# Inverse roots of two norms as columns on GpSimd, spread back by a product with ones, in a two-block transformer kernel

## What is computed

```python
# first block: after the two attentions (8 heads of 64 each)
y = jnp.concatenate([rmsnorm(merge(ya, DIL_WIDTH), g_out_dil[l]),
                     rmsnorm(merge(yb, MOBA_WIDTH), g_out_moba[l])], axis=-1)
h = h + y @ w_out[l]

# second block, in each of three mixers (layer 0 for c and x, layer 1 for x)
def layer_norm(x, g, b):
    mu = jnp.mean(xf, axis=-1, keepdims=True)
    var = jnp.mean(jnp.square(xf - mu), axis=-1, keepdims=True)
    y = (xf - mu) * lax.rsqrt(var + EPS)
    return (y * g + b).astype(x.dtype)

def conformer_conv(a, conv_w, conv_b, norm_g, norm_b, w_o):
    gl = a[..., :CONV_WIDTH_2] * jax.nn.sigmoid(a[..., CONV_WIDTH_2:])
    y = conv(gl, 31 taps per channel) + conv_b
    y = jax.nn.silu(layer_norm(y, norm_g, norm_b))
    return y @ w_o
```

## Time and profile before

| | |
|---|---|
| median of 3 runs | 2044.1 us |
| the profiled execution | 2042.34 us |
| its span, first to last instruction | 2040.5 us |
| mean granted TensorE clock | 0.992 of full speed |
| PE busy | 1979.1 us, 97% |
| DVE busy | 1657.4 us, 81% |
| ACT busy | 1114.2 us, 55% |
| GpSimd busy | 142.7 us, 7% |
| the chain that ended last | PE 72%, issue 14%, DVE 9%, ACT 5% |

### The profile page before, as it was taken

One profiled execution on the slowest core, in us unless ns is written; L12 is line 12 of the kernel. 1 busy time (PEld: TensorE's weight loads), 2 busy tenths in 40 slices (PEclk: granted clock), 3 DMA queues, 4 the chain that ended last, 5 costly groups with the idle time before them and its releaser, 6 DMA issues.

```text
span 2040.5 us, 29620 instructions
## 1 busy us (share of the span) xinstructions
PE 1979.1 (97%) x11323; PEld 1694.8 (83%) x11323; DVE 1657.4 (81%) x2464; ACT 1114.2 (55%) x1535; POOL 142.7 (7%) x258
## 2 busy tenths in 40 slices
PE   7999989999999999999999999999999999998998
PEld 6877889988878778888778888888888887787886
DVE  5877779888989987988987888877888889876665
ACT  5555454455674365577347645454665773365553
POOL 4000000000004000002300000000000013000000
PEclk9999999999999999999999999999999999998999
DMA  8635476677656656556656676777766566554653
GB/s 268 202 123 193 153 221 207 196 234 236 206 169 195 201 171 214 183 156 190 211 168 203 200 247 229 239 244 227 249 221 194 176 190 203 186 187 126 213 177 123
DMA packets 196716, 404.64 MB, mean 198 GB/s; under 512 B 15767, under 2 KB 18067, under 8 KB 196576
## 3 DMA queue, kind: packets, MB, share of 16 engines
q1 hardware_dynamic: 187888, 387.50, 59.8%
q0 software_dynamic: 8688, 15.25, 2.5%
HBM read 396.74 MB, written 1.10 MB: 195 GB/s over the span
## 4 chain that ended last, share of the span: by engine, by line
PE 72%; issue 14%; DVE 9%; ACT 5%; DMA 1%; POOL 0%; DVEq 0%; POOLq 0%; ACTq 0%
PE gps L1229 13%; PE gps L1231 13%; PE gps L1230 13%; PE gps L1253 6%; PE gps L1236 4%; PE gps L1237 4%; PE gps L1238 4%; PE gps L1255 3%; DVE wlo L2163 2%; PE gps L1213 2%; PE aps L1165 2%; PE aps L1131 2%; ACT whi L1634 1%; PE aps L1005 1%; PE aps L1118 1%
## 5 line engine op out<-in xcount | busy, mean ns | idle before, releaser
L2163 DVE TENSOR_TENSOR wlo<-raw,whi 128x1024 fp32r<-128x1024 f32 (+1 forms) x648 | 760.6, 1186 | 238.9 <-ACT whi L1634 236.1
L1634 ACT ACTIVATE whi<-raw 128x1024 fp32r<-128x1024 f32 (+1 forms) x648 | 660.6, 1027 | 529.1 <-PE gps L1231 377.8
L1229 PE MATMUL gps<-whi,both 128*128 128x512 f32 x1624 | 649.1, 400 | 6.8 <-DVE wlo L2163 6.6
L1231 PE MATMUL gps<-whi,both 128*128 128x512 f32 x1624 | 634.1, 390 | 0.0
L1230 PE MATMUL gps<-wlo,both 128*128 128x512 f32 x1624 | 633.9, 390 | 0.0
L1229 PEld LDWEIGHTS gps<-whi,both 128*128 128x128 f32 x1624 | 305.6, 188 | 79.9 <-DVE wlo L2163 11.6
L1231 PEld LDWEIGHTS gps<-whi,both 128*128 128x128 f32 x1624 | 305.5, 188 | 65.4
L1230 PEld LDWEIGHTS gps<-wlo,both 128*128 128x128 f32 x1624 | 305.8, 188 | 60.5
L1236 PE MATMUL gps<-both,whi 128*128 128x256 f32 x960 | 276.1, 288 | 1.5 <-DVE wlo L2163 1.5
L1237 PE MATMUL gps<-both,whi 128*128 128x256 f32 x960 | 271.7, 283 | 0.0
L1238 PE MATMUL gps<-both,wlo 128*128 128x256 f32 x960 | 271.6, 283 | 0.0
(11 more groups left out here) (314 smaller groups left out, 1759.9 us busy)
## 6 DMA issues: line engine op xcount, KB each, us to landing
raw<-w_in SPq DMA_DIRECT2D x232, 512.0 KB, 4.3
raw<-w_ff SPq DMA_DIRECT2D x192, 512.0 KB, 4.6
raw<-ada_wT SPq DMA_DIRECT2D x96, 512.0 KB, 4.4
raw<-w_attn_o SPq DMA_DIRECT2D x24, 512.0 KB, 4.3
raw<-w_gmlp_o SPq DMA_DIRECT2D x24, 512.0 KB, 3.8
raw<-w_conv_o SPq DMA_DIRECT2D x24, 512.0 KB, 3.8
raw<-w_out SPq DMA_DIRECT2D x24, 512.0 KB, 4.7
raw<-w_gate SPq DMA_DIRECT2D x20, 512.0 KB, 4.9
```

The source lines that it names most:

```text
L1229: mm(om, ah, whi[:, q, i, :], start=first, stop=False)
L1231: t = mm(om, al, whi[:, q, i, :], start=False, stop=last)
L1634: A_(part(whi, jb, q), raw_part(jb, q), ACT.Copy).then_inc(hi_done[q], 1)
L2163: tt(part(wlo, jb, q), raw_part(jb, q), f32(part(whi, jb, q)), ALU.subtract).then_inc(lo_done[q], 1)
```

## The change

The inverse root is taken on columns: PE forms the sums with the squares as the stationary side and two columns of ones as the moving side, so that a row's sum lands on its own partition; DVE adds EPS; GpSimd takes the power -0.5 of two columns (one per 128 rows); DVE writes two diagonal matrices from them (times D); and PE's product of the ones matrix with the diagonals spreads the values over all partitions again, into PSUM, from where DVE's scalings read them. In the first block `ynD` (diagonals) and `ynB` (spread and scaling) are new steps and `ynL` moves; in the mixers `ln_dg` and `ln_bc` are new, and the chain's steps from `ln_mu` to the last `ln_lo` lie later by a unit or two. One semaphore, `root_step`, counts four steps per root.

```diff
@@ make_plan, first block
         put(hosts[2], 2, "ynS", half=group)
         put(hosts[2], 3, "ynM", half=group)
-    put(j_km0, 2, "ynL", slot=2, half=0)
+        put(hosts[2], 3, "ynD", half=group)
+    put(j_km0, 0, "ynB", half=0)
+    put(j_km0, 1, "ynL", slot=2, half=0)
...
-    put(j_oa[0], 1, "ynL", slot=2, half=1)
+    put(j_oa[0], 1, "ynB", half=1)
+    put(j_oa[0], 2, "ynL", slot=2, half=1)
@@ mixer
-        lm = put(bg[1], 2, "ln_mu", l=l, cks=cks, rb_free=("t_pe", t_g, 4, 4))
-        put(bg[1], 3, "ln_mean", of=lm)
-        put(gates[4], 1, "ln_var", of=lm)
-        put(gates[4], 2, "ln_norm", of=lm)
+        lm = put(bg[1], 3, "ln_mu", l=l, cks=cks, rb_free=("t_pe", t_g, 4, 4))
+        put(gates[4], 0, "ln_mean", of=lm)
+        put(gates[4], 2, "ln_var", of=lm)
+        put(gates[4], 3, "ln_norm", of=lm)
+        put(gates[4], 3, "ln_dg", of=lm)
+        put(gates[5], 0, "ln_bc", of=lm)
         lo = []
-        for h, (at_out, at_mul, at_hi, at_lo) in enumerate((((gates[4], 2), (gates[4], 3), (gates[4], 3), (gates[5], 0)),
-                                                            ((gates[5], 0), (gates[5], 1), (gates[5], 1), (gates[5], 2)))):
+        for h, (at_out, at_mul, at_hi, at_lo) in enumerate((((gates[4], 3), (gates[5], 0), (gates[5], 0), (gates[5], 1)),
+                                                            ((gates[5], 1), (gates[5], 2), (gates[5], 2), (gates[5], 3)))):
@@ GpSimd
+            def root(k):
+                pool.wait_ge(sem["root_step"], 4 * k + 1)
+                nc.gpsimd.tensor_tensor(st[:, 15, 2:4], st[:, 15, 0:2], half_power[:], ALU.pow).then_inc(sem["root_step"], 1)
@@ TensorE, yn_sum
-                for k in range(4):
-                    t = mm(aps[:, 2, 0:S], ones[:], AB[:, k * S:(k + 1) * S], start=k == 0, stop=k == 3)
+                for m in range(2):
+                    for k in range(4):
+                        t = mm(aps[:, 2, 2 * m:2 * m + 2], AB[:, k * S + m * P:k * S + m * P + P], ones[:, 0:2],
+                               start=m == 0 and k == 0, stop=m == 1 and k == 3, skip_group_check=True)
                 t.then_inc(sem["yn_ss"], 1)
+            def spread(diagonals):
+                for m in range(2):
+                    t = mm(aps[:, 2, m * P:m * P + P], ones[:], diagonals[:, m * P:m * P + P], start=m == 0, stop=m == 1,
+                           skip_group_check=True)
+                return t
+            def yn_spread(p):
+                free(p)
+                pe.wait_ge(sem["root_step"], 4 * p.half + 3)
+                spread(GB).then_inc(sem["root_step"], 1)
@@ TensorE, ln_norm
-                ln_total(p, 1).then_inc(sem["ln_vs"], 1)
+                wait(pe, ev("ln_pc", p.of, 2, 2))
+                for m in range(2):
+                    t = mm(aps[:, 2, S + 2 * m:S + 2 * m + 2], PTb[:, 3 * S + m * P:3 * S + m * P + P], ones[:, 0:2], start=m == 0,
+                           stop=m == 1, skip_group_check=True)
+                t.then_inc(sem["ln_vs"], 1)
+            def ln_spread(p):
+                pe.wait_ge(sem["root_step"], 4 * p.of.n + 11)
+                spread(PTb).then_inc(sem["root_step"], 1)
@@ VectorE, first block
+            def diagonals(to):
+                for m in range(2):
+                    t = ts(to[:, m * P:m * P + P], ident[:], st[:, 15, 2 + m:3 + m], float(D), ALU.mult, ALU.mult)
+                return t
+            def yn_mean(p):
+                dve.wait_ge(sem["yn_ss"], p.half + 1)
+                ts(st[:, 15, 0:2], aps[:, 2, 0:4:2], 2.0, EPS, ALU.mult, ALU.add).then_inc(sem["root_step"], 1)
+            def yn_diagonals(p):
+                dve.wait_ge(sem["tp_st"], 16)
+                dve.wait_ge(sem["root_step"], 4 * p.half + 2)
+                diagonals(GB).then_inc(sem["root_step"], 1)
             def yn_scale(p):
-                ts(x, aps[:, 2, 0:S], 2.0 * CUBIC, EPS * CUBIC, ALU.mult, ALU.add).then_inc(sem["yn_ms"], 1)
-                dve.wait_ge(sem["yn_ms"], p.half + 1)
-                rsqrt(rs, x, t_)
+                dve.wait_ge(sem["root_step"], 4 * p.half + 4)
                 for k in range(4 * p.half, 4 * p.half + 4):
                     y = RB[:, k * S:(k + 1) * S]
-                    t = stt(y, y, C1[:, 16 + k:17 + k], rs, ALU.mult, ALU.mult)
+                    t = stt(y, y, C1[:, 16 + k:17 + k], aps[:, 2, 0:S], ALU.mult, ALU.mult)
@@ VectorE, mixers
             def ln_norm(p):
                 wait(dve, ev("ln_vs", p.of))
-                link(ts(x, aps[:, 2, S:2 * S], CUBIC, EPS * CUBIC, ALU.mult, ALU.add))
-                rsqrt(r, x, t_)
+                ts(st[:, 15, 0:2], aps[:, 2, S:S + 4:2], EPS, None, ALU.add).then_inc(sem["root_step"], 1)
+            def ln_diagonals(p):
+                dve.wait_ge(sem["root_step"], 4 * p.of.n + 10)
+                diagonals(PTb).then_inc(sem["root_step"], 1)
+            def ln_scale(p):
+                dve.wait_ge(sem["root_step"], 4 * p.of.n + 12)
+                r = aps[:, 2, 0:S]
                 for half in range(2):
                     y = tiles(Yc[:, half * 4 * S:(half + 1) * 4 * S], 4)
                     tt(y, y, r.unsqueeze(1).to_broadcast([P, 4, S]), ALU.mult).then_inc(sem["ln_n"], 1)
...
-            LATE = ("conv", "ynM", "rq", "rk", "gv_rms", "gv_norm", "final")
+            LATE = ("conv", "ynM", "ynD", "ln_dg", "rq", "rk", "gv_rms", "gv_norm", "final")
```

More of the change, by code:

```diff
@@ L573, in make_plan @@
             elif k == "ynM":
-                use(p, (2,), ("yn_ms", None, 0, p.half + 1))
+                use(p, (2,), ("root_step", None, 0, 4 * p.half + 1))
+            elif k == "ynB":
+                use(p, (2,), ("yn_y", None, 0, p.half + 1))
             elif k == "ma":
@@ L651 @@
 pn_ss pn_e pn_w po_e po_w pn_xn pn_xa t_pe t_hi t_lo
-ba_s ba_sb ba_nm ba_p ba_pn ba_tp ba_pt ba_pv ba_y yn_sq yn_ss yn_ms yn_y yn_hi yn_lo
+ba_s ba_sb ba_nm ba_p ba_pn ba_tp ba_pt ba_pv ba_y yn_sq yn_ss root_step yn_y yn_hi yn_lo
 ma_s ma_nm ma_p ma_pn ma_tp ma_pt ma_pv ma_hi ma_lo
@@ L949, in at_inverse, with yn_root, ln_root @@
                 nc.gpsimd.tensor_tensor(den[:, d0 + 6:d0 + 8], den[:, d0 + 4:d0 + 6], minus_one[:], ALU.pow).then_inc(sem["at_r"], 1)
-            stages = dict(atR=at_inverse, pn_stat=pn_root, po=po_root, wsT=ws_load, rep=copies, toep=toep, ba=ba, ctx_load=ctx_load, modT=mod_t, gb=gb, tab=tab)
+            def root(k):
+                pool.wait_ge(sem["root_step"], 4 * k + 1)
+                nc.gpsimd.tensor_tensor(st[:, 15, 2:4], st[:, 15, 0:2], half_power[:], ALU.pow).then_inc(sem["root_step"], 1)
+            def yn_root(p):
+                root(p.half)
+            def ln_root(p):
+                root(p.of.n + 2)
+            stages = dict(ynM=yn_root, ln_norm=ln_root, atR=at_inverse, pn_stat=pn_root, po=po_root, wsT=ws_load, rep=copies, toep=toep, ba=ba, ctx_load=ctx_load, modT=mod_t, gb=gb, tab=tab)
             for jb in jobs:
@@ L1194, in ln_norm @@
             def ln_norm(p):
-                ln_total(p, 1).then_inc(sem["ln_vs"], 1)
+                wait(pe, ev("ln_pc", p.of, 2, 2))
[6 more added lines that the diff above has]
+                spread(PTb).then_inc(sem["root_step"], 1)
             stages = dict(pp=pp, pp2=pp2, toep=toep, T=T, ba=ba, baT=baT, baV=baV, ynM=yn_sum, ma=ma, maT=maT, maV=maV,
                           tq=tq, tk=tk, at=at, atT=atT, atV=atV, spatial=spatial, wsT=ws_t, modT=mod_t,
-                          ck=ck, ln_mu=ln_mu, ln_mean=ln_mean, ln_var=ln_var, ln_norm=ln_norm)
+                          ck=ck, ln_mu=ln_mu, ln_mean=ln_mean, ln_var=ln_var, ln_norm=ln_norm, ln_bc=ln_spread, ynB=yn_spread)
             def unit(jb, q):
@@ L1829, in ba @@
                     t.then_inc(sem["ba_pn"], 1)
-            def yn_scale(p):
-                rs, x, t_ = GB[:, 0:S], GB[:, S:2 * S], GB[:, 2 * S:3 * S]
-                dve.wait_ge(sem["yn_ss"], p.half + 1)
-                dve.wait_ge(sem["tp_st"], 16)
-                ts(x, aps[:, 2, 0:S], 2.0 * CUBIC, EPS * CUBIC, ALU.mult, ALU.add).then_inc(sem["yn_ms"], 1)
-                dve.wait_ge(sem["yn_ms"], p.half + 1)
-                rsqrt(rs, x, t_)
+            def diagonals(to):
[9 more added lines that the diff above has]
+                diagonals(GB).then_inc(sem["root_step"], 1)
+            def yn_scale(p):
+                dve.wait_ge(sem["root_step"], 4 * p.half + 4)
                 for k in range(4 * p.half, 4 * p.half + 4):
                     y = RB[:, k * S:(k + 1) * S]
-                    t = stt(y, y, C1[:, 16 + k:17 + k], rs, ALU.mult, ALU.mult)
+                    t = stt(y, y, C1[:, 16 + k:17 + k], aps[:, 2, 0:S], ALU.mult, ALU.mult)
                 t.then_inc(sem["yn_y"], 1)
@@ L2006, in ln_lo @@
                     ALU.subtract).then_inc(sem["ln_lo"], 1)
-            stages = dict(pn_stat=pn_stat, final=final, po=po, T=T, pp_c=pp_c, ada=ada, ada2=ada, pp=pp, pp2=pp2, toep=toep, ba=ba, ynM=yn_scale, ynL=yn_lo, ma=ma,
```

(5 more changed lines are left out.)

1 line of the change is left out of this document (removed).

## The result

The changed kernel takes **2057.5 us** (median of 4 runs, 2056.7 to 2058.2) against 2044.1 of the kernel before beside it: ratio 1.0066, 95% interval 1.0054 to 1.0079, so 13.4 us slower (11.0 to 16.1). Run again beside other kernels it was 1.0070 (1.0057 to 1.0084). The profiled execution took 2057.9 us. The prediction was 2057.0 in a range of 2049.5 to 2065.

A forecast was written before the change was run, and what follows sets the result against it. TensorE (PE), busy 97% of 2040.5 us, was taken as the bound. Mixers +11.6 and first-block halves +1.2 and +0.1 made +12.9 on the profiled 2042.3, so 2055.2; 1.8 more to the median gave 2057.0, range 2049.5 to 2065.

The forecast's parts named there:

- The deciding fact: At the spreads, DVE reaches the diagonals 3.35 us after PE goes on; PE stands 4.04 us in each mixer.
- The power in the chain only in the first block: GpSimd's power adds 1.0 us to each first-block stand; in the mixers copy and split hide it.
- PE's own work: Narrow column sums taken as no change on PE; each of five spreads costs 0.5 us.
- The later chain: Mixers: stands of 5.7 us before the mean's sums and three of 0.36 go; 0.75 before the squares' sums comes, three times.
- The clock: Slow clock after each new stand taken at 1.4 us, bounds 0 and 3.4; one slow stretch of 1.7 us goes.
- The opposite rival: Two slow stretches for each new stand: up to +8 us, 2065; chance 0.12 together with slow narrow products.
- The relief of DVE: Eight DVE operations of 0.42 us saved at five places lie beside PE's products, worth nothing in a mixer.
- The credit of 8.5 for the later chain: Mixers: 5.7 us of stands, 1.7 of clock and three waits of 0.36 won by the chain one unit later.
- 3 us to spare: At the mixers' branch, the second low part is there at 19.5 us, where PE needs it at 22.5.
- The sum: Mixers +11.6 us, first block's half 0 +1.2 and half 1 +0.1, in all +12.9.
- Rival 2: Diagonals are made before PE asks, so all stands at the spreads go: -14 us, 2030; chance 0.05.

The follow-up runs named there:

- early diagonals: Changed kernel with the mean and diagonals of all five roots out of LATE, before the split of the next job's unit 3: 2034.0 us, ratio 0.9949.
- mixers_early: Kernel before with only the mixers' three roots new, the later chain, and their diagonals before the split: 2043.2 us against 2043.5, ratio 0.9997.
- mixers only: Changed kernel with the old root put back in the first block, new roots and later chain kept in the mixers: 2055.0 us, ratio 1.0049.
- no root: Changed kernel without the power on GpSimd, DVE making the diagonals straight from its own mean: 2054.5 us against 2043.5, ratio 1.0052.
- first_only: Changed kernel with the old chain and old root put back in the mixers, new roots only in the first block: 2044.5 us, ratio 1.0003.
- the later chain alone: Kernel before, its old root on DVE and no spread, with only the layer norm's chain one unit later: 2043.3 us against 2044.2, ratio 0.9996.
- first_early: New roots only in the first block, mean and diagonals before the split, mixers as before the change: 2034.7 us against 2044.0, ratio 0.9956.
- the later spread with early diagonals: Kernel with early diagonals, its layer norm spreads and the first of the first block's spreads one unit later: 2039.2 us, ratio 0.9980.

## Why the prediction was right

- **The deciding fact** (DVE reaches LATE of unit 3 too late, and the spread stands in front of unit 0): right, and shown by early diagonals. PE stands 3.71, 3.71, 3.70 in the mixers by the modelled end of the last product, or 3.9 from where the next could have started (products start 0.23 apart and are shown 0.40 long, so 0.17 more); predicted 4.04. DVE came to the diagonals 3.34 us after PE could have gone on (726.89 to 730.23), against 3.35 predicted; the step from there to the spread took 0.53 instead of 0.69. Half 0: 5.06 or 5.2, predicted 5.04. Half 1: 2.56 or 2.7, predicted 2.71.
- **The power in the chain only in the first block**: right for the changed kernel; it measures 0.99 and 0.81 where 1.0 was taken, and 0 in the mixers.
- **PE's own work**: the sixteen narrow records take 1.70 us to the next product (98.83 to 100.53), where the eight wide ones took 1.53 (98.29 to 99.82); taken as no change, +0.17. The Trainium skill's load price (TensorE: Matmul & The Clock Gate, section LDWEIGHTS (loading the stationary operand)), 107 ns for 128 columns, makes sixteen an estimate of 1.71, and the trace agrees. A spread is 0.36 us at full clock (early diagonals, 102.86 to 103.22), 0.46 in a mixer of `mixers_early`, and 0.84 at half (108.62 to 109.46); 0.5 was taken.
- **The later chain**: the stands before the mean's sums and the waits of 0.36 went, as said. The squares: 1.66, 0.50 and 0.50, so 2.7 for 2.25; in mixer 1 DVE still had steps of the adaptation (L1822) in front.
- **The clock**: mis-sized. 1.4 us were taken for each stand. In the mixers' three stands of 3.71, in four executions (the change twice, mixers only, no root), a slow stretch followed all twelve times. Seven were of 3.4 us, 1.7 lost. Five were of 6.8 us, of which 1.2 to 1.8 passed while PE still stood, so 2.5 to 2.8 were lost: 2.1 on average. The opposite rival (two stretches each) is what mixer 1 showed in the changed kernel. Behind half 1's stand of 2.56 us, where a fall was expected, the change's second execution and `first_only` show none.
- **The relief of DVE**, "worth nothing in a mixer": it held. In the changed kernel PE stands for the spread and reaches the branch 17.7 to 18.7 us after the mean, about 4 us behind the low parts, and without those stands `mixers_early` shows no gain from it either.
- **The credit of 8.5 for the later chain**: right in the changed kernel, and there alone. With the old root and no spread PE comes to the branch 11.75 us after the mean and finds the low parts late. The "3 us to spare" exist because PE stands at the spread first. The prediction doesn't say so, and my expectation for the later chain alone took the credit over and missed for that reason.
- **The sum**: +11.6 for the mixers, 11.9 by the stretches and +10.8 by the part alone; +1.3 for the first block, +0.3 by the part alone (interval -1.4 to +2.5). The two profiled executions tell the terms apart. PE's idle time grew by 8.3 us (69.7 against 61.4); the prediction's stands come to 8.2, with the shorter stands made up by the squares and the unforeseen L1054. PE's busy time grew by 7.2. Of this 4.7 is the clock (14.8 us lost against 10.1, estimated in the same way up to 1900 us; 0.4 of the difference lies at stands that the change doesn't touch), where the prediction has 2.2, and 2.5 is left for spreads and narrow sums, where it has 2.5. That makes 15.5 us against 12.9, and nearly the whole miss is the clock. The medians are 13.4 apart, nearer to the forecast, because the profiled execution of before was 1.8 us below its median and that of the change 0.4 above: this part of the agreement is chance.
- **Rival 2** (diagonals made before PE asks, -14, 2030) named the point that decides. Built on purpose it gives 2034, most of the 4 us between being the stands at the mixers' spreads (1.8), the small stands of 0.96 and 0.44 at L1054 in the first block, and the squares in mixer 1; with DVE's order mended as well it is 2029.9.

## What to carry to other kernels

Before a product is made to depend on another engine, find where that engine is in its own queue when the product is reached; an operation of 0.5 us placed behind a split cost 3.7 us of PE, and the same operation in front of it nothing or 0.6. When a wait vanishes, look whether the data came earlier or the waiting engine later: in the mixers the low parts came no earlier with the new root, PE only arrived 1.2 us later. A stand removed at one step is worth only as much as the next step of the same chain has in reserve. In the first block the new root in front of the split won 9 us; how much of that is the shorter work of DVE and how much its place was not told apart, since the old root was not tried in front of the split.

## What was not expected of the hardware

The slow clock does not follow from the length of the stand alone. Windows of the later spread with early diagonals, around or behind its three equal stands of 1.89 us (mixers 1, 2, 3; the first window holds its stand, which ends at 730.04):

```profile
728.00:732.00 4.00, 2.11 (x10) 1.67 (x10) 2.17 (x3) 3.97 (x7) 0.00 (x0) 1.00 0.39 131
1073.90:1077.30 3.40, 3.40 (x10) 2.62 (x10) 2.79 (x3) 3.05 (x4) 0.00 (x0) 0.55 0.16 61
1794.00:1797.40 3.40, 3.40 (x10) 2.67 (x9) 2.80 (x3) 3.05 (x4) 0.00 (x0) 0.53 0.13 51
```

The first keeps the level of 2.4 GHz, the others fall. The two stands of 2.17 us before the mean's sums behave the other way round: in all three kernels that have them (before, `first_only`, `first_early`) the one in mixer 1 is followed by a slow stretch and the one in mixer 2 is not. A stand of 2.4 us near 1500 us, outside the change and the same in all fourteen kernels, is followed by 3.4 us at half clock in seven of them and by none in the other seven. And one stand of 5.06 us in the same place was followed by 3.4 us at half clock in the profiled execution of the changed kernel, and by 6.8 in the second execution of the same kernel and in `first_only`:

```profile
107.10:113.90 6.80, 5.87 (x28) 5.90 (x28) 2.33 (x6) 0.00 (x0) 0.76 (x2) 0.51 0.44 154
```

What decides between them was not found. It moves one execution by 0.9 to 1.7 us at each such place.
